# Final token half of a transformer trunk: last weights in two column halves, a square on VectorE, a 5 to 3 output scaling, one output transfer issued by ScalarE

## What is computed

```python
h = h + 0.5 * swiglu_ffn(h, ffn_norm[0, 0], ffn_w_in[0, 0], ffn_w_out[0, 0])
h = h + mlstm_mixer(rmsnorm(h, mix_norm[0]), ...)
h = h + 0.5 * swiglu_ffn(h, ffn_norm[0, 1], ffn_w_in[0, 1], ffn_w_out[0, 1])
return rmsnorm(h, final_norm)      # h * rsqrt(mean(h * h) + 1e-6) * gain
```

## Time and profile before

| | us |
|---|---|
| median of 3 runs | 1839.97 |
| lowest, highest | 1839.9, 1840.75 |
| the profiled execution, its own time | 1839.55 |
| its span, first to last instruction | 1837.5 |
| time outside its span | 2.05 |
| TensorE busy in the span | 1820.7 |
| last matmul begins | 1828.32 |
| last output transfer is issued | 1833.57 |

### The profile page before, as it was taken

How to read it: one execution, slowest core, us unless ns; L and a number is a source line. 1 busy time by engine, 2 the same in 40 slices (tenths; PEclk the granted TensorE clock), 3 DMA queues, 4 the chain that set the end, 5 groups by cost and what they waited for, 6 DMA issues and landing times.

```text
span 1837.5 us, 21636 instructions
## 1 busy us (share of the span) xinstructions
PE 1820.7 (99%) x8228; PEld 1506.1 (82%) x8228; DVE 1314.6 (72%) x1470; ACT 938.8 (51%) x1040; POOL 38.2 (2%) x52
## 2 busy tenths in 40 slices
PE   8999999999999999999999999999999999999998
PEld 6888888888888888888888888888888888888886
DVE  7888888888855554555477757888888888754444
ACT  6555555555654444444445445555555555653442
POOL 0000000000100000000000000000000000000000
PEclk9999999999999999999999999999999999999999
DMA  7666555665556565557645456666665566556664
GB/s 230 222 210 206 196 197 184 197 200 199 178 182 200 190 191 182 166 169 206 192 140 149 160 183 190 211 207 207 204 202 187 184 205 202 194 188 198 194 193 137
DMA packets 180607, 350.68 MB, mean 191 GB/s; under 512 B 10848, under 2 KB 11040, under 8 KB 180256
## 3 DMA queue, kind: packets, MB, share of 16 engines
q1 hardware_dynamic: 179952, 348.17, 59.3%
q0 software_dynamic: 432, 1.18, 0.3%
q10 hardware_dynamic: 128, 0.03, 0.0%
HBM read 347.24 MB, written 2.10 MB: 190 GB/s over the span
## 4 chain that ended last, share of the span: by engine, by line
PE 98%; DVE 1%; ACT 1%; issue 0%; DMA 0%; DVEq 0%; ACTq 0%
PE acc L426 49%; PE acc L490 8%; PE acc L488 8%; PE acc L489 8%; PE aux L490 7%; PE aux L488 7%; PE aux L489 7%; PE aux L483 1%; PE aux L455 1%; PE aux L699 1%; PE aux L649 0%; PE aux L687 0%; DMA h<-in_x_dram 0%; ACT sums L787 0%; ACT u_hi L765 0%
## 5 line engine op out<-in xcount | busy, mean ns | idle before, releaser
L1139 DVE TENSOR_TENSOR w_lo<-raw,w_hi 128x1024 fp32r<-128x1024 f32 x336 | 410.8, 1228 | 330.0 <-ACT w_hi L750 327.5
L750 ACT ACTIVATE w_hi<-raw 128x1024 fp32r<-128x1024 f32 x336 | 354.4, 1059 | 349.7 <-PE acc L426 339.7
L426 PE MATMUL acc<-w_hi,g_hi 128*128 128x512 f32 x704 | 274.9, 390 | 0.0
L426 PE MATMUL acc<-w_hi,g_lo 128*128 128x512 f32 x704 | 274.0, 389 | 0.0
L426 PE MATMUL acc<-w_lo,g_hi 128*128 128x512 f32 x704 | 273.9, 389 | 0.0
L426 PE MATMUL acc<-w_hi,u_hi 128*128 128x512 f32 x512 | 203.9, 398 | 2.8 <-DVE w_lo L1139 2.8
L426 PE MATMUL acc<-w_hi,u_lo 128*128 128x512 f32 x512 | 200.2, 391 | 0.0
L426 PE MATMUL acc<-w_lo,u_hi 128*128 128x512 f32 x512 | 200.2, 391 | 0.0
L1221 DVE TENSOR_TENSOR w_lo<-raw,w_hi 128x1024 fp32r<-128x1024 f32 x112 | 135.2, 1222 | 51.2 <-ACT w_hi L825 51.2
L825 ACT ACTIVATE w_hi<-raw 128x1024 fp32r<-128x1024 f32 x112 | 116.4, 1057 | 87.1 <-PE aux L490 46.1
L426 PEld LDWEIGHTS acc<-w_hi,g_lo 128*128 128x128 f32 x704 | 132.1, 188 | 27.4
(11 more groups left out here) (227 smaller groups left out, 3231.6 us busy)
## 6 DMA issues: line engine op xcount, KB each, us to landing
raw<-in_ffn_w_in_dram SPq DMA_DIRECT2D x248, 512.0 KB, 4.5
raw<-in_ffn_w_out_dram SPq DMA_DIRECT2D x176, 512.0 KB, 4.6
raw_more<-in_ffn_w_in_dram SPq DMA_DIRECT2D x104, 512.0 KB, 4.5
raw<-in_a_w_in_dram SPq DMA_DIRECT2D x96, 512.0 KB, 4.3
raw<-in_a_w_out_dram SPq DMA_DIRECT2D x32, 512.0 KB, 4.5
h<-in_x_dram SPq DMA_DIRECT2D x4, 512.0 KB, 8.8
final_gain<-in_final_norm_dram POOLq DMA_DIRECT2D x1, 1024.0 KB, 5.3
out_dram<-h SPq DMA_DIRECT2D x1, 1024.0 KB, 3.9
```

Of the source, the lines that this page charges most:

```text
L426: mm = nc.tensor.matmul(acc[:, TT * (c % 2) + t, :], s[:, k, tok], w[:, ring, kk, :], start=(k == 0 and n == 0), stop=(k == GK * granules ...
L750: nc.scalar.activation(w_hi[:, n % RING], raw[:, n % RING], ACT.Copy)\
L1139: nc.vector.tensor_tensor(w_lo[:, n % RING], raw[:, n % RING], w_hi[:, n % RING].bitcast(F32), ALU.subtract)\
```

## The change

- **TensorE.** In block n = 3, the sum of t = 1 in `acc` is closed after 18 of the 22 granules (`early`). The last four granules of t = 1 are multiplied in two column halves of 256, into `aux[0]` and then `aux[1]`: 24 matmuls of 256 columns each, and a `last_summed` signal after each half.
- **VectorE.** As soon as the 18 granules are summed, it adds half of that sum to `h` into `sums[:, 2]`. The work of t = 0 stands unchanged behind that. For t = 1 it adds half of each 256-column half to `sums[:, 2]`. Behind the first of the two it waits for ScalarE's square and folds all sums of squares known so far, the division and the small constant into `known_sq`. Behind the second it squares the second half itself (`last_sq`), adds the two in one instruction, and goes to the same inverse root.
- **ScalarE** squares only the first 256 columns of `tile` for t = 1. It scales columns 1280 to 2047 (768 of them), and issues their output transfer itself.
- **VectorE** scales columns 0 to 1279 (`VEC_END`), and SyncE issues their transfer.
- **GpSimd** multiplies the last block of t = 1 by the gain in two halves.

```diff
+    VEC_END = 5 * D // 8
...
+        known_sq = sb("known_sq", [P, 1])
+        last_sq = sb("last_sq", [P, 1])
...
             load_out(1)
-            half = D // 2
             sp.wait_ge(vec_out, 1)
             sp.dma_start(out_tokens[:, 0, :], h[:, 0, :]).then_inc(out_stored, 16)
             sp.wait_ge(vec_out, 2)
-            sp.dma_start(out_tokens[:, 1, 0:half], h[:, 1, 0:half]).then_inc(out_stored, 16)
-            sp.wait_ge(act_out, 1)
-            sp.dma_start(out_tokens[:, 1, half:], h[:, 1, half:]).then_inc(out_stored, 16)
+            sp.dma_start(out_tokens[:, 1, 0:VEC_END], h[:, 1, 0:VEC_END]).then_inc(out_stored, 16)
             sp.wait_ge(out_stored, 48)
...
             pool.wait_ge(final_gain_landed, 16)
             for n in range(ND):
                 cols = slice(n * COLS, (n + 1) * COLS)
-                for t in range(TT):
+                for t in range(TT if n < ND - 1 else 1):
                     if n == ND - 1:
-                        pool.wait_ge(last_ready, t + 1)
+                        pool.wait_ge(last_ready, 1)
                     elif t == 0:
                         pool.wait_ge(tile_ready, R_H3 + n - R_HID1 + 1)
                     last = nc.gpsimd.tensor_tensor(h[:, t, cols], tile[:, t, :], final_gain[:, cols],
                                                    ALU.mult)
                     if n == ND - 1 or t == TT - 1:
                         last.then_inc(kept, 1)
+            for half in range(2):
+                pool.wait_ge(last_ready, 2 + half)
+                at, cols = slice(half * SEQ, (half + 1) * SEQ), slice(D - (2 - half) * SEQ, D - (1 - half) * SEQ)
+                nc.gpsimd.tensor_tensor(h[:, 1, cols], tile[:, 1, at], final_gain[:, cols], ALU.mult)\
+                    .then_inc(kept, 1)
         @block.tensor
...
-            def matmuls(c, ring, k, kk, t, granules, s_hi, s_lo):
+            def matmuls(c, ring, k, kk, t, granules, s_hi, s_lo, early=False):
                 tok = slice(t * P, (t + 1) * P)
+                end = GK * (granules - RING if early and t else granules) - 1
                 for n, (s, w) in enumerate(((s_hi, w_hi), (s_hi, w_lo), (s_lo, w_hi))):
                     mm = nc.tensor.matmul(acc[:, TT * (c % 2) + t, :], s[:, k, tok], w[:, ring, kk, :],
                                           start=(k == 0 and n == 0),
-                                          stop=(k == GK * granules - 1 and n == 2))
+                                          stop=(k == end and n == 2))
                 return mm
-            def run(c, g, more, first, last, granules, s_hi, s_lo, need=None):
+            def run(c, g, more, first, last, granules, s_hi, s_lo, need=None, early=False):
                 for i in range(first, last):
...
                     ring = (g + i) % RING
                     for kk in range(GK):
                         for t in range(TT):
-                            mm = matmuls(c, ring, GK * i + kk, kk, t, granules, s_hi, s_lo)
+                            mm = matmuls(c, ring, GK * i + kk, kk, t, granules, s_hi, s_lo, early)
                     mm.then_inc(granules_used, 1)
             def turn(r, more, half, src=None, ps=None):
...
                 for n in range(1, ND):
                     if n >= 2:
                         pe.wait_ge(tile_ready, R_H3 + n - 2 - R_HID1 + 1)
-                    run(c + n, g + n * GF, 0, 0, GF if n < ND - 1 else GF - RING, GF, g_hi, g_lo)
+                    run(c + n, g + n * GF, 0, 0, GF if n < ND - 1 else GF - RING, GF, g_hi, g_lo,
+                        early=n == ND - 1)
                 g += (ND - 1) * GF
-                for t in range(TT):
+                for i in range(GF - RING, GF):
+                    pe.wait_ge(low_ready, g + i + 1)
+                    for kk in range(GK):
+                        mm = matmuls(c + ND - 1, (g + i) % RING, GK * i + kk, kk, 0, GF, g_hi, g_lo)
+                mm.then_inc(last_summed, 1)
+                for half in range(2):
+                    at = slice(half * SEQ, (half + 1) * SEQ)
                     for i in range(GF - RING, GF):
-                        if t == 0:
-                            pe.wait_ge(low_ready, g + i + 1)
                         for kk in range(GK):
-                            mm = matmuls(c + ND - 1, (g + i) % RING, GK * i + kk, kk, t, GF, g_hi, g_lo)
+                            k, ring = GK * i + kk, (g + i) % RING
+                            mm = product(aux[half][:, 0:SEQ], g_hi[:, k, T1], g_lo[:, k, T1],
+                                         w_hi[:, ring, kk, at], w_lo[:, ring, kk, at],
+                                         k == KF - GK * RING, k == KF - 1)
                     mm.then_inc(last_summed, 1)
...
                 elif r < R_H3 + ND - 1:
                     act.wait_ge(tile_ready, r - R_HID1 + 1)
                 for t in range(TT):
+                    width = COLS
                     if r == R_H3 + ND - 1:
                         act.wait_ge(last_ready, t + 1)
-                    src = h[:, t, n * COLS:(n + 1) * COLS] if r is None else tile[:, t, :]
+                        width = COLS if t == 0 else SEQ
+                    src = h[:, t, n * COLS:(n + 1) * COLS] if r is None else tile[:, t, 0:width]
                     done = TT * (ND * norm + n) + t
                     if done:
                         act.wait_ge(squared, done)
-                    nc.scalar.activation(scratch[:, :], src, ACT.Square,
+                    nc.scalar.activation(scratch[:, 0:width], src, ACT.Square,
                                          accum_out=squares[:, norm, t, n:n + 1]).then_inc(squared, 1)
             def silu_first(i):
...
             ffn_out(1)
             square(3, ND - 1, R_H3 + ND - 1)
             act.wait_ge(rstd_ready, 5)
-            act.wait_ge(kept, 3 * ND + 1)
-            nc.scalar.activation(h[:, 1, D // 2:], h[:, 1, D // 2:], ACT.Copy, scale=rstd[:, 3, 1:2])\
+            act.wait_ge(kept, 3 * ND + 2)
+            nc.scalar.activation(h[:, 1, VEC_END:], h[:, 1, VEC_END:], ACT.Copy, scale=rstd[:, 3, 1:2])\
                 .then_inc(act_out, 1)
+            act.wait_ge(act_out, 1)
+            act.dma_start(out_tokens[:, 1, VEC_END:], h[:, 1, VEC_END:]).then_inc(out_stored, 16)
         @block.vector
...
             c, last_cols = C_FFN_OUT[1] + ND - 1, slice((ND - 1) * COLS, D)
             dve.wait_ge(squared, TT * (4 * ND - 1))
             dve.wait_ge(kept, 3 * ND - 1)
-            for t in range(TT):
-                dve.wait_ge(last_summed, t + 1)
-                nc.vector.scalar_tensor_tensor(out=tile[:, t, :], in0=acc[:, TT * (c % 2) + t, :],
-                                               scalar=0.5, in1=h[:, t, last_cols],
-                                               op0=ALU.mult, op1=ALU.add).then_inc(last_ready, 1)
-                rms(3, t, t + 1)
-                dve.wait_ge(rstd_ready, 4 + t)
-                dve.wait_ge(kept, 3 * ND + t)
-
-                cols = slice(0, D if t == 0 else D // 2)
-                nc.vector.tensor_scalar(h[:, t, cols], h[:, t, cols], rstd[:, 3, t:t + 1], None,
-                                        ALU.mult).then_inc(vec_out, 1)
+            bank = acc[:, TT * (c % 2):TT * (c % 2) + TT, :]
+            dve.wait_ge(granules_used, G_FFN_OUT[1] + ND * GF - RING)
+            link(nc.vector.scalar_tensor_tensor(out=sums[:, 2, :], in0=bank[:, 1, :], scalar=0.5,
+                                                in1=h[:, 1, last_cols], op0=ALU.mult, op1=ALU.add))
+            dve.wait_ge(last_summed, 1)
+            nc.vector.scalar_tensor_tensor(out=tile[:, 0, :], in0=bank[:, 0, :], scalar=0.5,
+                                           in1=h[:, 0, last_cols], op0=ALU.mult, op1=ALU.add)\
+                .then_inc(last_ready, 1)
+            rms(3, 0, 1)
+            dve.wait_ge(rstd_ready, 4)
+            dve.wait_ge(kept, 3 * ND)
+            nc.vector.tensor_scalar(h[:, 0, :], h[:, 0, :], rstd[:, 3, 0:1], None, ALU.mult)\
+                .then_inc(vec_out, 1)
+
+            for half in range(2):
+                at = slice(half * SEQ, (half + 1) * SEQ)
+                dve.wait_ge(last_summed, 2 + half)
+                nc.vector.scalar_tensor_tensor(out=tile[:, 1, at], in0=aux[half][:, 0:SEQ], scalar=0.5,
+                                               in1=sums[:, 2, at], op0=ALU.mult, op1=ALU.add)\
+                    .then_inc(last_ready, 1)
+                if half == 0:
+                    dve.wait_ge(squared, TT * ND * 4)
+                    link(nc.vector.tensor_reduce(known_sq[:, :], squares[:, 3, 1:2, :], AXX, ALU.add))
+                    link(nc.vector.tensor_scalar(known_sq[:, :], known_sq[:, :], 1.0 / D, EPS, ALU.mult,
+                                                 ALU.add))
+            dve.wait_ge(last_ready, 3)
+            link(nc.vector.scalar_tensor_tensor(out=sums[:, 1, 0:SEQ], in0=tile[:, 1, SEQ:], scalar=1.0,
```

(9 more changed lines are left out.)

## The result

The changed kernel takes 1866.97 us as the median of 4 runs (1866.41 to 1867.41), the one before 1839.93 (1839.49 to 1840.75). The ratio is 1.0146, with a 95% interval of 1.0134 to 1.0158. The forecast was 1840.8 with a range to 1841.6. It was wrong by 26 us, far outside.

A forecast was written before the change was run, and what follows sets the result against it. TensorE, busy 99% of the span, was taken as the bound, so only the tail could change: +0.25 (VectorE order) +0.43 (GpSimd) +0.14 (first issue) = +0.82, from 1839.97 to 1840.8 us, range 1839.4 with 0.2 scatter to 1841.6.

The forecast's parts named there:

- The bound of 0.5%: Tail after TensorE's last piece: all the change can win or lose lies in 8.8 us, 0.5% of the time.
- What no row shows: Leftover chance of 0.03 for outcomes outside the forecast and rivals, a third of it a gain.
- any shift before 1817: Sign that the forecast is wrong: timings in the trace move ahead of 1817 us, before the tail.
- Matmuls of 256 columns 0.1185 apart: TensorE, last granules of t = 1: 48 matmuls take 5.69 against 5.44 us, ending 0.25 later, hidden by VectorE's order.
- rival (3): TensorE tail: 256-column matmuls do not overlap the next weight load; second residual 6.9 later, about 1847.7 us; chance 0.03.
- First residual on the heels of the scaling: VectorE, first half of t = 1: residual starts when t = 0's scaling ends, 1828.34, and takes 0.45 us.
- The adding instruction held 0.43 by GpSimd: VectorE tail: the one-column, two-input add meets GpSimd's multiplication and loses 0.43 us, bounds 0 and 0.64.
- Rival (1): VectorE tail: GpSimd does not hold up the short adding instruction; +0.39, 1840.4 us; chance 0.27.
- The final scaling 0.68 late: End of t = 1: the inverse root begins 0.68 us late, putting the final scaling at 1833.07 against 1832.39.
- The landing 0.82 late: Last output transfer: the first issue comes 0.82 us later, and the end hangs on that first issue.
- Transfers of two queues share one rate: Output of t = 1: both transfers count as one megabyte, landing 3.9 us after the first issue.
- rival (2): Output transfers: two queues do not share one rate, 640 KB lands 2.93 after issue; 1839.4 to 1839.8 us; chance 0.2.

The follow-up runs named there:

- tail_reordered: Changed kernel with its new tensors allocated last, one-tensor-input adding instruction, second residual and square ahead of the wait for ScalarE; 1839.93 us against 1840.36 for the kernel before.
- tensors_last: Changed kernel with its two new one-column tensors allocated behind all others; 1840.36 us against 1840.22 for the kernel before the change, ratio 1.0001.

## Why the prediction was wrong

**The step that failed** is the one before the sum: "All that can be won or lost by a change in this tail lies in 1837.5 - 1828.7 = 8.8 us, 0.5% of the time." The part-by-part reading took the two lines that allocate `known_sq` and `last_sq` as free and gave them no term at all. They moved all that is allocated behind them by 64 bytes, and that cost 26 us, spread over the matmuls of the whole span. The bound of 0.5% held for the instructions, not for the addresses. "What no row shows" had been given 3%, and the range no room. The last sentence of the prediction named "any shift before 1817" as what would prove it wrong; that is what came.

**The steps in the tail** held, with these sizes:

- Matmuls of 256 columns 0.1185 apart: 0.114 measured in the changed kernel, 0.120 at the old distance. In both, the 48 of them fit between the end of t = 0 and the second residual and never held VectorE up, as forecast. So rival (3), loads that do not overlap, is out. In `tail_reordered`, where nothing else is late, TensorE is.
- The early sum hidden: yes, the 0.68 of it lies in front of an idle 2.69.
- First residual on the heels of the scaling, at 1.29 behind its start: measured 1.20 (1855.54 - 1854.34), since it starts a little before the scaling ends. It took 0.42, the lower of the two figures that I had, where I took 0.45.
- ScalarE's square and handover for 256 columns 0.53: 0.54 (1856.53 - 1855.99).
- From the root's start to the scaling 1.79: 1860.21 - 1858.42 = 1.79.
- The adding instruction held 0.43 by GpSimd: 0.40 (0.56 against 0.16), of which 0.35 left with the second tensor input. (Read one by one, the 3.25 of the earlier trace rows is 1.22 and 1.98, and GpSimd's 1.23 shows no wait: there VectorE's second subtraction alone was held, which changes nothing in the sum.) Rival (1), no wait, is out.
- The final scaling 0.68 late by the sum, 0.53 measured. Of the 0.15 too much, 0.09 is the earlier start of the first residual; the rest lies in 0.01 to 0.03 for each of four later steps.
- The landing 0.82 late by the sum: 10.73 - 10.02 = 0.71.
- Transfers of two queues share one rate. The stretches of `tensors_last`, issues at 1835.09 and 1835.14:

```profile
1836.00:1836.50 0.50, 0.00 (x0) 0.00 (x0) 0.00 (x0) 0.00 (x0) 0.00 (x0) 0.50 1.01 420
...
1838.00:1838.50 0.50, 0.00 (x0) 0.00 (x0) 0.00 (x0) 0.00 (x0) 0.00 (x0) 0.50 0.92 356
1838.50:1839.00 0.50, 0.00 (x0) 0.00 (x0) 0.00 (x0) 0.00 (x0) 0.00 (x0) 0.50 0.10 31
```

The engines are full to the end, and the last landing is 3.95 after the first issue, against 3.90 before. SyncE's 640 KB landed 3.7 after their issue, not 2.93. So rival (2) is out too.

With the tensors in their old places the forecast of 1840.8 stands against a measured 1840.36 (1839.93 to 1841.5). That does not rescue it: the kernel asked about was the other one. And the agreement says little, since these times can't tell a loss of 0.8 from none; the 0.7 is shown by the rows of the tail alone.

## What to carry to other kernels

An edit that allocates memory has a part of its own in the working: list what is allocated behind it, and ask which pairs of stationary and moving tensors change their distance. In this kernel it was enough to put the new small tensors behind the large ones, or to fill up to 256 bytes. When a kernel gets slower, compare first a stretch that the change does not touch.

## What was not expected of the hardware

- Matmuls with 128 x 128 fp32r weights and 512 moving columns went 227 ns apart (median) when stationary and moving tensor lay a multiple of 256 bytes apart, and 232 to 234 when the stationary one lay 32, 64 or 128 bytes ahead, at the same granted clock of 1.00. At 64 bytes the mean cost of a g matmul was 6.5 ns, 2.9%, and the spacing was 0.232 us with all other engines idle.
- It depends on the sign: 64 bytes ahead cost 5.8 to 6.5 ns, 64 bytes behind 1.6 to 2.8.
- It depends on the width: with 256 moving columns the 64 bytes made the spacing shorter, 114 ns against 120.
- No distance tried was faster than 227 ns for 512 columns. Why the distance matters was not shown, and matmuls of another type were not tried.
